# Sharing a scatter between two DMA queues: the regrouping copies of a long convolution's forward transform, partly issued by SyncE

## The reference, cut to what matters

```python
def bidir_long_conv(z, h_fwd, h_bwd, bias):
    L = z.shape[1]
    k = jnp.concatenate([h_fwd, jnp.zeros_like(h_fwd[:1]), h_bwd[1:][::-1]], axis=0)
    kf = jnp.fft.rfft(k.astype(jnp.float32), n=2 * L, axis=0)
    zf = jnp.fft.rfft(z.astype(jnp.float32), n=2 * L, axis=1)
    y = jnp.fft.irfft(zf * kf, n=2 * L, axis=1)[:, :L]
    return (y + z.astype(jnp.float32) * bias).astype(z.dtype)
...
    z = v
    for n, gate in enumerate((x1, x2)):
        z = gate * bidir_long_conv(z, filt[:, n, 0], filt[:, n, 1], fbias[n])
```

## Time and profile before

| | us |
|---|---|
| median of three runs | 3408.88 (3405.33 to 3414.22) |
| profiled execution, its own time | 3408.59 |
| its span, first to last instruction | 3406.9 |
| PE busy in the span | 3183.0 (93%) |
| POOL busy in the span | 313.0 (9%) |
| mean granted TensorE clock | 0.972 of full speed |

### The profile page before, as it was taken

The page is one execution under the profiler, slowest core; times in us unless marked ns, Lnnn a source line. Parts: engine busy times, 40 slices in busy tenths (PEclk is TensorE's granted clock), DMA queues, the critical chain, the costliest instruction groups (busy, mean ns, idle before and its releaser), DMA issues.

```text
span 3406.9 us, 49323 instructions
## 1 busy us (share of the span) xinstructions
PE 3183.0 (93%) x19122; PEld 2488.8 (73%) x19122; DVE 2163.4 (64%) x3218; ACT 1290.3 (38%) x2124; POOL 313.0 (9%) x508
## 2 busy tenths in 40 slices
PE   7999979998898999999999889999999899999897
PEld 3888645555676888888787757777778578888785
DVE  6989855555467555455767656666566666566766
ACT  3221333333335323333445444444343353333344
POOL 0111245544100000000000200000000000000000
PEclk8999999999898999999999999999999999999999
DMA  7655656678512223225434410000012143334532
GB/s 293 207 201 200 220 164 186 188 193 222 176 63 86 81 81 99 78 81 202 150 98 158 146 59 17 21 12 17 12 31 81 50 142 96 105 108 166 178 102 87
DMA packets 186046, 413.78 MB, mean 121 GB/s; under 512 B 33695, under 2 KB 60639, under 8 KB 183143
## 3 DMA queue, kind: packets, MB, share of 16 engines
q1 hardware_dynamic: 133640, 274.23, 24.7%
q0 software_dynamic: 51936, 131.27, 12.8%
q10 hardware_dynamic: 288, 5.77, 0.4%
HBM read 262.90 MB, written 81.00 MB: 101 GB/s over the span
## 4 chain that ended last, share of the span: by engine, by line
PE 76%; DVE 12%; DMA 4%; ACT 3%; issue 3%; POOL 1%; SPq 1%; DVEq 0%; ACTq 0%; POOLq 0%
PE ps L660 19%; PE ps L661 19%; PE ps L662 19%; PE ps L2510 2%; PE ps L2528 2%; PE ps L2619 2%; PE ps L2384 2%; PE ps L730 2%; PE ps L2584 1%; PE ps L2549 1%; PE ps L2580 1%; DMA traw<-hidden_scratch 1%; DMA t2k<-s 1%; PE ps L2593 1%; DVE mx L2995 1%
## 5 line engine op out<-in xcount | busy, mean ns | idle before, releaser
L660 PE MATMUL ps<-HB,gsp 128*128 128x512 f32 x1232 | 488.1, 396 | 37.1 <-DVE HB L836 21.9
L661 PE MATMUL ps<-HB,gsp 128*128 128x512 f32 x1232 | 484.6, 393 | 0.0
L662 PE MATMUL ps<-HB,gsp 128*128 128x512 f32 x1232 | 483.2, 392 | 0.0
L1121 DVE TENSOR_TENSOR gsp<-graw,gsp 128x512 fp32r<-128x512 f32 x330 | 226.4, 690 | 262.4 <-ACT gsp L1100 261.6
L1100 ACT ACTIVATE gsp<-graw 128x512 fp32r<-128x512 f32 x330 | 206.6, 628 | 326.4 <-PE ps L662 266.6
L660 PEld LDWEIGHTS ps<-HB,gsp 128*128 128x128 f32 x1232 | 234.1, 190 | 90.3 <-issue 21.4
L662 PEld LDWEIGHTS ps<-HB,gsp 128*128 128x128 f32 x1232 | 233.9, 190 | 49.8
L661 PEld LDWEIGHTS ps<-HB,gsp 128*128 128x128 f32 x1232 | 234.3, 190 | 46.5 <-issue 1.0
L660 PE MATMUL ps<-tsp,wdh 128*128 128x512 f32 x616 | 242.9, 394 | 18.3 <-DVE tsp L1382 18.3
L662 PE MATMUL ps<-tsp,wdh 128*128 128x512 f32 x616 | 241.5, 392 | 0.0
L661 PE MATMUL ps<-tsp,wdh 128*128 128x512 f32 x616 | 241.4, 392 | 0.0
(11 more groups left out here) (288 smaller groups left out, 7265.3 us busy)
## 6 DMA issues: line engine op xcount, KB each, us to landing
graw<-in_w_gu SPq DMA_DIRECT2D x176, 256.0 KB, 2.7
mring<-in_mod_w POOLq DMA_DIRECT2D x78, 512.0 KB, 4.7
hidden_scratch<-R SPq DMA_DIRECT2D x154, 256.0 KB, 2.4
traw<-hidden_scratch SPq DMA_DIRECT2D x154, 256.0 KB, 2.7
t2k<-s POOLq DMA_DIRECT2D x80, 256.0 KB, 5.9
t2z<-s POOLq DMA_DIRECT2D x160, 128.0 KB, 3.8
t2w<-w POOLq DMA_DIRECT2D x160, 128.0 KB, 3.3
wraw<-in_w_in SPq DMA_DIRECT2D x48, 256.0 KB, 4.4
```

Source lines behind the costliest of these rows:

```text
L660: pe.matmul(o, wh, xh, start=start, stop=False, skip_group_check=onto)
L661: pe.matmul(o, wh, xl, start=False, stop=False, skip_group_check=onto)
L662: return pe.matmul(o, wl, xh, start=False, stop=stop, skip_group_check=onto)
L1121: dve.tensor_tensor(gsp[U % 3][:, 1, :], graw[:, q, W_SLOT[i], :], gsp[U % 3][:, 0, :].bitcast(F32), ALU.subtract).then_inc(w.lo, 1)
```

## The change

The last piece (u = 3) of a latent share's Y is scattered by SP instead of POOL: four DMAs. In the context's Y, SP issues the two scatters of each piece that go to the upper half of the partitions (h = 1), POOL the two of the lower half. The Z steps stay with POOL. SP's scatters raise a semaphore of their own, `s_s1h`, and `sent` and ACT's wait for a slot also wait for it. In the latents' Y, SP issues the scatters ahead of its own waits and loads of that step.

```diff
@@ -546,6 +546,7 @@
+        s_s1h = sem("s1_slot_sent_by_sp")
@@ -1725,6 +1726,7 @@
+        SP_SENT = []
@@ -1737,7 +1739,9 @@
-            S1_SENT += {"K": [("K", 2)] * 2, "Z": [("Z", 4)] * 4, "Y": [("Z", 4)] * 4}.get(kind, [])
+            S1_SENT += {"K": [("K", 2)] * 2, "Z": [("Z", 4)] * 4,
+                        "Y": [("Z", 4)] * 3 + [("Z", 0)] if it < NCH else [("Z", 2)] * 4}.get(kind, [])
+            SP_SENT += {"K": [0] * 2, "Z": [0] * 4, "Y": [0] * 3 + [4] if it < NCH else [2] * 4}.get(kind, [])
@@ -1771,6 +1775,8 @@
             for slot in range(4):
                 if s1_sent(uses, slot):
                     eng.wait_ge(s_s1o[slot], s1_sent(uses, slot))
+            if sum(SP_SENT[:uses]):
+                eng.wait_ge(s_s1h, 16 * sum(SP_SENT[:uses]))
@@ -1793,6 +1799,11 @@
+        def signal_scatter(eng, it, u, b, h, c, sent_by=None):
+
+            eng.dma_start(landing(t2z, it, h, c, u if it < NCH else 0, 0 if it < NCH else CW * u, CW),
+                          s1[b % 4][:, CW * (2 * h + c):CW * (2 * h + c + 1)]).then_inc(sent_by or s_s1o[b % 4], 16)
@@ -1942,7 +1953,16 @@
-                elif kind == "Y" and it < NCH:
+                elif kind == "Y" and it == NCH:
+                    for u in range(4):
+                        sp.wait_ge(s_be, n["B"] + u + 1)
+                        for c in range(2):
+                            signal_scatter(sp, it, u, n["B"] + u, 1, c, s_s1h)
+                elif kind == "Y":
+                    sp.wait_ge(s_be, n["B"] + 4)
+                    for c in range(2):
+                        for h in range(2):
+                            signal_scatter(sp, it, 3, n["B"] + 3, h, c, s_s1h)
                     sp.wait_ge(s_ae, A_END["Y", it, 1])
                     sent(sp, B_END["Y", it, 1])
                     sp.dma_start(share(gbuf, it), u_share(it, 1)).then_inc(s_gl, 16)
@@ -2046,8 +2066,8 @@
                         for c in range(2):
                             for h in range(2):
-                                pool.dma_start(landing(t2z, it, h, c, u if it < NCH else 0, 0 if it < NCH else CW * u, CW),
-                                               s1[b % 4][:, CW * (2 * h + c):CW * (2 * h + c + 1)]).then_inc(s_s1o[b % 4], 16)
+                                if kind == "Z" or (u < 3 if it < NCH else h == 0):
+                                    signal_scatter(pool, it, u, b, h, c)
@@ -2150,6 +2170,8 @@
                 if b >= 4:
                     act.wait_ge(s_s1o[b % 4], s1_sent(b, b % 4))
+                    if SP_SENT[b - 4]:
+                        act.wait_ge(s_s1h, 16 * sum(SP_SENT[:b - 3]))
```

## The result

| | before | after |
|---|---|---|
| median on the same chips, 16 runs each, us | 3413.52 (3405.33 to 3417.72) | 3420.75 (3413.49 to 3430.31) |
| profiled execution's span, us | 3406.9 | 3420.2 |
| POOL busy, us | 313.0 | 300.2 |
| mean granted TensorE clock | 0.972 | 0.970 |

The change makes the kernel slower: the ratio of the times is 1.0025, 95% interval 1.0018 to 1.0032, or 8.5 us (6.1 to 10.9) on 3408.6. The forecast was 8.8 us the other way. The two profiled executions stand 13.3 us apart, more than the medians; I use them to see where time goes, and the ratios for how much.

A forecast was written before the change was run, and what follows sets the result against it. TensorE's own work was taken as three quarters of the span, with 24.6 us of PE idle time in reach. Gains of 2.3 + 0.9 + 1.5 + 1.6 + 0 + 2.5 = 8.8 us off 3408.59 gave 3399.8 us, range 3393 to 3409.

The forecast's parts named there:

- What M waits for: Second M of each share: it waits for the signal's scatters only, with PE idle 24.6 us together.
- Rival 4: Second M of each share: M really waited for something else and nothing moves, 3408.6 us; chance 0.06.
- POOL's issue ends 2.35 us sooner: Latents' Y: POOL issues 12 scatters instead of 16, 0.59 us each, so it is through 2.35 us earlier.
- the gains of 0.9 and 1.5 us: M in shares 1 and 2: idle time won back, limited by the next filter transform's need of DVE's result.
- 588.5, or 5.9 us after ACT's end: Share 1's Y: landing of SP's last scatter, with 0.6 us an issue and 1.7 us added for busy engines.
- Rival 3: Latents' last piece: SP lands later than POOL did, on half the engines; 5.1 us slower, 3413.7 us; chance 0.07.
- The clock in share 2: Behind share 2's M: without most of the idle time the granted clock no longer falls, a gain of 1.6 us.
- Share 3, 0: Share 3's Y: the DMA engines are the bound at 102% busy, so the gain is 0.
- The context, 2.5 us: Context's Y: gain from two issuers, taken half way between 0.5 us and 4.4 us.
- rival 1: Engines, not queues, are full: context gains 0.5 us, the clock's fall stays; 5.2 us gained, 3403.4 us; chance 0.25.
- The covers: Share 1: ACT's added slot wait is covered by some 7 us and counts 0; SP's loads move with the landings.
- The range: Whole kernel: time from 3393 to 3409 us, leaving out rival 3.

The follow-up runs named there:

- hold_filter: `latents_only` with POOL holding back the filter scatters that follow Y until SP's four signal scatters have landed; ratio to the kernel before 1.0029.
- sp_alone: `hold_filter` with SP's four scatters of the last piece also held back until POOL's twelve have landed; ratio to the kernel before 1.0069.
- sixteen_rows: `latents_only` with each of SP's four scatters going to 16 partitions with 8 runs instead of 8 with 16; ratio to the kernel before 1.0040.
- busy_wait: `latents_only` with twelve throwaway matmuls on PE ahead of the wait at the latents' second M; ratio to the kernel before 1.0011.
- context_only: The kernel after with the latents' last piece given back to POOL, SP keeping its context scatters; ratio to the kernel before 1.0000.
- piece_one: The kernel after with SP scattering the latents' second piece (u = 1) instead of the last, the context all POOL's; ratio to the kernel before 1.0019.
- latents_only: The kernel after with all context scatters given back to POOL, SP keeping the latents' last piece; ratio to the kernel before 1.0040.
- half_of_last: The kernel after with SP issuing only two of the latents' last piece's four scatters (c = 1), the context all POOL's; ratio to the kernel before 1.0008.
- after_filled: The kernel after with throwaway matmuls ahead of every M and 18 short ones ahead of the context's B; ratio to the kernel before 1.0028.
- before_filled: The kernel before with throwaway matmuls ahead of every M and 18 short ones ahead of the context's B; ratio to the kernel before 0.9995.

## Why the prediction was wrong, step by step

- **What M waits for: right.** M stands 0.2 to 0.4 us behind the gate load, which waits for the same landings, in all latent shares before and after, and the name t2k in the rows was an accident of the inference: holding these copies back (`hold_filter`) did not free M. Rival 4 is out.
- **POOL's issue ends 2.35 us sooner: right in share 0 only**, 1.33 us in shares 1 and 2. Its last scatter was to land at 587.5, 4.9 us behind ACT's end; `sp_alone` has it 6.6 us behind in share 1 and 6.4 in share 2 with nothing beside. One microsecond of that is the later issue, the rest the way from last issue to landing, 4.1 us in share 1 (587.86 to 591.96) for 3.5. So of the gains of 0.9 and 1.5 us in these shares only some 0.5 and 1.1 were there to be had.
- **"588.5, or 5.9 us after ACT's end" for SP's landing: wrong; this is the step that failed.** It took the landing from SP's copies in the attention and added 1.7 us for engines 71% busy. Alone the piece takes 5.2 to 5.6 us (`sp_alone`), so the base, 4.2 us, was short by a microsecond or more. In company it is 9.0 to 9.8, so the allowance should have been 3.4 to 4.5 us. The 0.6 us an issue was also wrong in company: 0.95 to 1.17.
- **Rival 3, chance 0.07: what happened.** It put M 9.4 us behind ACT's end; measured 9.43, 10.17, 9.98 and 8.85 in shares 0 to 3. Its 5.1 us stand against 5.9. Its point of decision, 7.3 us, was passed in every share. Its reason, half of the engines at half rate, 74 GB/s, is not what happened: by itself SP's queue moved 143 GB/s, and `sixteen_rows` was no faster. Its size came out right for another reason, company on the engines; that is luck. I held against it POOL's own 267 GB/s, but that is the rate of the queue that was already flowing, and says nothing of what a second queue gets.
- **The clock in share 2, "1.6 us more": wrong in sign.** The mechanism was right in the main, that idle time ahead of M can bring the clock down behind it (`busy_wait`). Being the other way round, it added up to 5.2 us in the profile instead of giving 1.6 back, and in shares 0 and 1 above all. But `context_only` kept its clock behind 2.10 us in share 2 and lost it behind 1.95 in share 1, with nothing changed there, so even a shorter wait would not have made the 1.6 us safe. A forecast that counts a gain from the clock owed rival 3 the loss from it: 5.9 + 5.2 = 11.1 us in these profiles instead of 5.1.
- **Share 3, 0: right** (+0.12 us).
- **The context, 2.5 us: wrong, rival 1 right.** 150 GB/s where it had been 148, and a ratio of 1.0000; the 223 GB/s of Z did not come. The Trainium skill (DMA: Bandwidth & Descriptors, Rules for kernel authors) has it that disjoint halves serialise on the same engines, and this case agrees: halfway between two rows was no reasoning where one row showed full engines.
- **The covers: as predicted.** The slot is written again at 602.14 in share 1, 7 us behind the landing and released by PE (only `piece_one` made ACT wait), and SP's loads moved with the landing.
- **The range** ended at 3409; the ratio on 3408.6 gives 3417.1. It left out rival 3 and the clock on top of it. The loss of 0.25% is smaller than the 0.3% that the prediction thought a measurement could tell, but the sixteen runs tell it.

**The cause.** Shown: the loss is in the latents' last piece; SP's scatters take 5.2 to 5.6 us by themselves and 9.0 to 9.8 beside POOL's; neither issue time, nor number of rows, nor later filter copies (in shares 1 and 2), nor which of the pieces explain it; and the clock behind the wait is a large part of the loss. Argued only: how the engines share themselves between the queues. In the context's rows POOL's 1.05 MB go in the 256 packets of over 2 KB, 4 KB each, and SP's 1.05 MB in 1280 - 256 = 1024 of 1 KB, so turns taken packet by packet would give SP's queue less; 2 KB runs should then have helped and didn't. The uneven tail of `hold_filter` suggests that single engines with a backlog set the end. The two were not told apart. Nor do the runs say why POOL's first scatter of Y goes out a microsecond later in shares 1 and 2, or why `latents_only` and the last 3.4 us of the profile lose more than these terms.

## What to carry to other kernels

Before a transfer on the critical path goes to a second queue, ask what the engines do at that moment: time saved in issuing is worth something only if the last landing comes sooner, and a piece that started on an idle queue beside a flowing one took 9.0 to 9.8 us here, against 5.2 to 5.6 alone. Price such a landing from a row in which both queues flow, or leave the last piece where its queue is already flowing. And where an engine's idle time grows by microseconds ahead of matmuls, price the clock behind it too: here it was up to as much as the wait. Read it from more than one profiled execution: which share lost its clock changed between two kernels with the same latent code.

## What the runs showed of the hardware that was not expected

- SP's issue of a 128 KB scatter takes 0.66 to 0.69 us when POOL issues nothing (2.63 to 2.77 us for four, `sp_alone`), and 0.95 to 1.17 us for four in a row beside POOL (3.81 to 4.67 us, shares 0 to 2 after). Two in a row beside POOL took 1.32 us in share 1 of `half_of_last`, 0.66 each.
- Data of SP's queue first moved some 2.6 us after the first issue beside POOL's flow (`hold_filter`, share 1), and 1.3 us after it alone (`sp_alone`, share 1).
- Behind ACT's last piece of share 1 one queue moved 204 GB/s and two together 202.
- In company the first queue is late as well: POOL's last piece landed 6.9 us behind its last issue in `piece_one`, share 1, where it had been 3.2.
- Two queues in the context moved 150 GB/s together with the engines full; one had moved 148.
- In `sp_alone` the queue by itself moved 143 GB/s at 43.8% of the engines' time, so more could flow beside it; beside POOL's copies its 0.31 MB went at 82 GB/s.
- Twelve throwaway matmuls in a wait kept the granted clock at full speed behind it (1.00 in both windows shown; M to S 24.2 to 24.3 us in all four shares). Ahead of the context's B eighteen short ones did so where they left no idle time (1.00, 7.36 us for 64 matmuls, `after_filled`), and did not where 1.13 us were left (0.50, 13.24 us, `before_filled`).
- The granted clock fell behind idle times of 1.95 and 2.94 us in `context_only` and of 2.09 us in share 2 of the kernel before, and stayed at 1.00 behind 2.10 and 3.03 us in the same two kernels.
